# The first of five input pieces projected without its norm, and the norm applied to its 272 columns as products leave PSUM

## What is computed

```python
def rmsnorm(x, g):
    y = x32 * lax.rsqrt(jnp.mean(x32 * x32, axis=-1, keepdims=True) + EPS)
    return (y * g).astype(x.dtype)

def mixer(h, cos, sin, p):          # h = rmsnorm(input, ln_mix_g)
    proj = h @ p['w_in']
    q, k, v, xr, yg = jnp.split(proj, ...)
    q, k = rope(q), rope(k)         # then windowed attention
    xc = centred_depthwise_conv(xr, ...)   # then two gated scans
...
for l in range(DEPTH):
    h = h + mixer(rmsnorm(h, p['ln_mix_g']), cos, sin, p)
    h = h + hier_moe(rmsnorm(h, p['ln_ffn_g']), p)
```

## Time and profile before

| | us |
|---|---|
| median of 3 runs | 1206.02 (1204.71 to 1206.12) |
| the profiled execution | 1203.64 |
| its span, first to last instruction | 1201.9 |
| TensorE busy | 1151.7 (96%) |
| VectorE / ScalarE busy | 925.4 (77%) / 841.1 (70%) |
| mean granted clock of TensorE | 0.985 |

### The profile page before, as it was taken

One profiled execution on the slowest core, in us unless ns is written; L12 is line 12 of the kernel. 1 busy time (PEld: TensorE's weight loads), 2 busy tenths in 40 slices (PEclk: granted clock), 3 DMA queues, 4 the chain that ended last, 5 costly groups with the idle time before them and its releaser, 6 DMA issues.

```text
span 1201.9 us, 21054 instructions
## 1 busy us (share of the span) xinstructions
PE 1151.7 (96%) x5977; PEld 987.8 (82%) x5977; DVE 925.4 (77%) x1254; ACT 841.1 (70%) x1041; POOL 243.5 (20%) x261
## 2 busy tenths in 40 slices
PE   7999999998999999989999999999999999999992
PEld 6999999977888888877788788888888888888881
DVE  6768887476777778679887965566888888888886
ACT  7538888586666666566777855556877777777775
POOL 2130001100111111122232322222322322322320
PEclk8999999999999999999999999999999999999996
DMA  9540111462333322448999787878999999999978
GB/s 350 200 133 18 44 45 34 108 189 78 99 105 93 85 85 85 189 162 332 402 383 375 285 318 255 300 257 292 387 372 378 379 372 363 380 378 366 395 295 326
DMA packets 73271, 291.23 MB, mean 242 GB/s; under 512 B 15051, under 2 KB 30796, under 8 KB 48642
## 3 DMA queue, kind: packets, MB, share of 16 engines
q1 hardware_dynamic: 53826, 257.42, 56.1%
q0 software_dynamic: 19392, 33.16, 10.9%
HBM read 267.75 MB, written 37.62 MB: 254 GB/s over the span
## 4 chain that ended last, share of the span: by engine, by line
PE 80%; DMA 9%; DVE 5%; issue 2%; ACT 2%; SPq 1%; POOL 0%; DVEq 0%; ACTq 0%; POOLq 0%
PE ps L2451 26%; PE ps L800 14%; PE ps L2494 13%; PE ps L1462 9%; DMA raw_w_gate<-in_w_gate 6%; PE ps L1414 3%; PE ps L822 2%; PE ps L1380 2%; PE ps L2438 2%; PE ps L563 2%; PE ps L1391 2%; PE ps L1440 1%; PE ps L2485 1%; DMA raw_w_up<-in_w_up 1%; ACT g_hi L2557 1%
## 5 line engine op out<-in xcount | busy, mean ns | idle before, releaser
L2661 DVE TENSOR_TENSOR d_lo<-raw_w_down,d_hi 128x2048 fp32r<-128x2048 f32 x62 | 139.8, 2289 | 46.9 <-ACT d_hi L2557 46.9
L2661 DVE TENSOR_TENSOR g_lo<-raw_w_gate,g_hi 128x2048 fp32r<-128x2048 f32 x64 | 144.9, 2289 | 35.3 <-ACT g_hi L2557 35.0
L2661 DVE TENSOR_TENSOR u_lo<-raw_w_up,u_hi 128x2048 fp32r<-128x2048 f32 x64 | 143.8, 2288 | 6.5 <-ACT u_hi L2557 6.3
L2557 ACT ACTIVATE g_hi<-raw_w_gate 128x2048 fp32r<-128x2048 f32 x64 | 120.6, 1912 | 25.1 <-DMA raw_w_gate<-in_w_gate 17.9
L2557 ACT ACTIVATE u_hi<-raw_w_up 128x2048 fp32r<-128x2048 f32 x64 | 120.0, 1910 | 10.3 <-DMA raw_w_up<-in_w_up 10.0
L2557 ACT ACTIVATE d_hi<-raw_w_down 128x2048 fp32r<-128x2048 f32 x62 | 115.9, 1910 | 5.8 <-DMA raw_w_down<-in_w_down 5.8
L2494 PE MATMUL ps<-d_hi,hid_hi 128*128 128x512 f32 x272 | 110.7, 407 | 0.4 <-DVE hid_lo L2690 0.4
L2494 PE MATMUL ps<-d_lo,hid_hi 128*128 128x512 f32 x272 | 106.8, 393 | 0.0
L2494 PE MATMUL ps<-d_hi,hid_lo 128*128 128x512 f32 x272 | 106.4, 391 | 0.0
L800 PE MATMUL ps<-h_hi,w_hi 128*128 128x432 f32 (+2 forms) x304 | 104.8, 345 | 0.8 <-DVE h_lo L634 0.8
L800 PE MATMUL ps<-h_lo,w_hi 128*128 128x432 f32 (+2 forms) x304 | 104.3, 343 | 0.0
(11 more groups left out here) (397 smaller groups left out, 2772.2 us busy)
## 6 DMA issues: line engine op xcount, KB each, us to landing
raw_w_gate<-in_w_gate SPq DMA_DIRECT2D x64, 1024.0 KB, 11.5
raw_w_up<-in_w_up SPq DMA_DIRECT2D x64, 1024.0 KB, 11.9
raw_w_down<-in_w_down SPq DMA_DIRECT2D x62, 1024.0 KB, 11.8
w_raw<-in_w_in SPq DMA_DIRECT2D x14, 512.0 KB, 3.6
xh<-in_x SPq DMA_DIRECT2D x10, 512.0 KB, 3.2
h_dram<-xh SPq DMA_DIRECT2D x10, 512.0 KB, 4.2
u_dram<-u SPq DMA_DIRECT2D x10, 512.0 KB, 4.8
k_win<-k_dram POOLq DMA_DIRECT2D x12, 384.0 KB, 5.5
```

The lines of the kernel that those rows point to most:

```text
L2557: act.activation(hi[c][:, :], raw[c][:, :], ACT.Copy).then_inc(hi_done, 1)
L2661: dve.tensor_tensor(lo[c][:, :], raw[c][:, :], hi[c][:, :].bitcast(F32), ALU.subtract).then_inc(lo_done, 1)
```

## The change

Piece 0 is no longer scaled. ScalarE rounds `h_f * g` directly (`first_hi`), VectorE takes the rest (`first_lo`), and TensorE multiplies these. VectorE keeps the row of rstd for the 272 columns in SBUF (`keep_rstd`, in the first columns of `k_pre`; k itself moves to `feat[:, 1, :]`) and multiplies by it wherever a product's first 272 columns leave PSUM: two of `first_scale`, one `scaled_out_of` for each of the tiles 2 to 11, two of `late_scaled` for tiles 12 and 13. ScalarE's copies of those chunks begin at column 272. Chunk 2 of each tile waits for that tile's `scaled_out`, since it writes the same bank, and so do the third and fourth late products.

The loads start with the transposed input of piece 0 and the weights of tile 0; the token rows come in the order t = 3, 4, 0, 1, 2, 5 and so on (`ORDER` = pieces 1, 0, 2, 3, 4). On TensorE the transposes move too. Since `first_rstd` lies in memory that mask buffer 0 takes later, the mask of the first block is loaded later, after the first `swap_q`.

```diff
+    ORDER = (1, 0, *range(2, PIECES))
+    TILE_ORDER = [t for c in ORDER for t in tiles_of(c)]
...
-        load_x(0)
-        load_x(1)
-        load_x(2)
+        sp.dma_start(g_rows[:, :], a["mix_col"]).then_inc(xt_arrived[0], 16)
+        load_xt(0)
+        sp.dma_start(w_raw[0][:, :, :], a["w_in"][0]).then_inc(w_arrived[0], 16)
+        load_x(3)
+        load_x(4)
         sp.dma_start(ident[:, :], a["ident"]).then_inc(consts_in, 16)
-        sp.dma_start(g_rows[:, :], a["mix_col"]).then_inc(consts_in, 16)
-        load_xt(0)
-        for f in range(2):
-            sp.dma_start(w_raw[f][:, :, :], a["w_in"][f]).then_inc(w_arrived[f], 16)
-        for c in range(1, PIECES):
+        sp.dma_start(w_raw[1][:, :, :], a["w_in"][1]).then_inc(w_arrived[1], 16)
+        load_xt(1)
+        for t in tiles_of(0):
+            load_x(t)
+        for c in range(2, PIECES):
             load_x(2 * c + 1)
             load_x(2 * c + 2)
             load_xt(c)
...
+        def first_hi(j):
+            for k in range(HALVES[j].start, HALVES[j].stop):
+                ins = act.activation(h_hi[:, k, piece_cols(0)], h_f[:, k, piece_cols(0)], ACT.Copy, scale=g_rows[:, k:k + 1])
+            ins.then_inc(h_hi_done, 1)
...
-        for t in tiles_of(0):
-            norm(t, t % 2)
-        for j in range(2):
-            split_w(j, j, 0)
-            hi_half(0, j)
+        act.wait_ge(xt_arrived[0], xt_count(0))
+        first_hi(0)
+        split_w(0, 0, 0)
+        first_hi(1)
         for t in tiles_of(1):
-            norm(t, t % 2)
+            norm(t)
+        split_w(1, 1, 0)
         for c in range(1, PIECES):
-            if c >= 2:
+            if c >= 3:
                 first_output(c - 2, 0)
+            if c == 1:
+                norm(0)
+                norm(1)
+                for j in range(2):
+                    hi_half(c, j)
+                norm(2)
...
+    def late_scaled(dve, j):
+        f, bank, _ = late_at(j)
+        dve.wait_ge(proj_out, PUT - len(LATE) + j + 1)
+        dve.tensor_tensor(feat[:, 2 * FT - FTILES + f, META:FIRST_END], bank[:, 0:FIRST_END - META], first_rstd[:, META:FIRST_END],
+                          ALU.mult).then_inc(scaled_out, 1)
...
+        def first_lo(j):
+            dve.wait_ge(h_hi_done, done(j))
+            for k in range(HALVES[j].start, HALVES[j].stop):
+                cols = piece_cols(0)
+                ins = dve.scalar_tensor_tensor(out=h_lo[:, k, cols], in0=h_f[:, k, cols], scalar=g_rows[:, k:k + 1],
+                                               in1=h_hi[:, k, cols].bitcast(F32), op0=ALU.mult, op1=ALU.subtract)
+            ins.then_inc(h_lo_done, 1)
+
+        def keep_rstd():
+            dve.wait_ge(x_turned, done(ORDER.index(0)))
+            dve.tensor_copy(first_rstd, tr[0][:, 0, 0:FIRST_END]).then_inc(first_scaled, 1)
+
+        def first_scale(f):
+            dve.wait_ge(proj_done, f + 3)
+            dve.wait_ge(first_scaled, 1)
+            dve.tensor_tensor((k_own, v_pre)[f][:, 0:FIRST_END], ps[:, FIRST_BANKS[0][f], 0:FIRST_END], first_rstd,
+                              ALU.mult).then_inc(first_scaled, 1)
+
+        def scaled_out_of(f):
+            s = f % 2
+            bank = ps[:, (NCH * s) % 2, :]
+            if f in WITH_META:
+                ft = (f - X0) // 2
+                dve.wait_ge(proj_out, NCH * f + 3)
...
+                dve.tensor_tensor(one(xr, ft, 2 + OFF1, 2 + OFF1 + META), bank[:, 0:META], first_rstd[:, 0:META], ALU.mult)
+                dve.tensor_tensor(one(xr, ft, 2, 2 + FIRST_END), bank[:, 0:FIRST_END], first_rstd, ALU.mult).then_inc(scaled_out, 1)
+            else:
+                scaled_feat(dve, f, bank)
...
         def tile(f, s):
...
                 pe.wait_ge(proj_out, NCH * f + c + 1)
+                if c == 2:
+                    pe.wait_ge(scaled_out, scaled_by(f))
                 third(s, c, (NCH * s + c) % 2, cols=tile_cols(f, c))
...
-        spread(0)
         first_piece(0)
         spread(1)
         first_piece(1)
+        spread(0)
+        piece(0, 1)
         spread(2)
-        for c in range(1, PIECES):
-            for f in range(2):
-                piece(f, c)
-            if c + 2 < PIECES:
-                spread(c + 2)
+        piece(1, 1)
+        for c in range(2, PIECES):
+            piece(0, c)
+            if c + 1 < PIECES:
+                spread(c + 1)
+            piece(1, c)
         tile(X0, 0)
...
         def first_step():
+            projected["late_scaled"](dve, 0)
+            projected["late_scaled"](dve, 1)
             rope_q(0, 0)
```

More of the change, by code:

```diff
@@ L429, in put @@
                 cols = tile_cols(FTILES - 1, c)
-                return act.activation(feat[:, j, cols], bank[:, 0:cols.stop - cols.start], ACT.Copy)
+                lo_ = FIRST_END if c == 0 else cols.start
+                return act.activation(feat[:, j, lo_:cols.stop], bank[:, lo_ - cols.start:cols.stop - cols.start], ACT.Copy)
             return put
@@ L438, in put @@
                 if c == 0:
-                    piece(2 + OFF1, bank, 0, META)
-                    return piece(2, bank, 0, CH)
+                    return piece(2 + FIRST_END, bank, FIRST_END, CH - FIRST_END)
                 if c == 1:
@@ L639, in split_w @@
                               ALU.subtract).then_inc(w_lo_done, 1)
[L641 to L646 removed]
+        dve.wait_ge(xt_arrived[0], xt_count(0))
+        first_lo(0)
         split_w(0, 0)
[L648 removed]
+        first_lo(1)
         for t in tiles_of(1):
             spread_rstd(t)
+        split_w(1, 1)
         for c in range(1, PIECES):
             scale_piece(c)
[L653 to L657 removed]
+            if c == 1:
+                spread_rstd(0)
+                spread_rstd(1)
+                lo_half(c, 0)
+                lo_half(c, 1)
+                spread_rstd(2)
+                keep_rstd()
+                for t in tiles_of(2):
+                    spread_rstd(t)
+                first_scale(0)
+            else:
+                if c < PIECES - 1:
+                    for t in tiles_of(c + 1):
+                        spread_rstd(t)
+                lo_half(c, 0)
+                lo_half(c, 1)
+            if c == 2:
+                first_scale(1)
         step = [0]
@@ L699, in convolve @@
                                          in1=conv, op0=ALU.mult, op1=ALU.add).then_inc(conv_step if j < 3 else conv_done, 1)
+                if j == 2 and f:
+                    scaled_out_of(f)
         def split_xc(ft):
@@ L761, in rec_step @@
             split_w(2 * k + X0 + 3 + d, 1 - d)
-            if d == 1 and not (isinstance(k, int) and k == FT - 1):
-                convolve(k + 1)
+            if d == 1 and k < FT - 1:
+                convolve(k + 1, 2 * k + X0 + 3)
+            elif d == 1:
+                scaled_out_of(2 * k + X0 + 3)
             decayed(k, d)
@@ L1175, in _ @@
         sp.wait_ge(projected["proj_out"], put - late + 2)
+        sp.wait_ge(*projected["scaled_out"])
         swap_q(0)
+        sp.wait_ge(*projected["first_tables"])
+        sp.sem_inc(tables_in[0], 32)
+        sp.dma_start(mask[0][:, :], a["masks"][0]).then_inc(tables_in[0], 16)
         tables(1, 1)
@@ L1746, in rope_q @@
             if isinstance(t, int) and t == 0:
-                dve.wait_ge(projected["proj_out"], put - late + 2)
+                dve.wait_ge(*projected["scaled_out"])
+                dve.wait_ge(*projected["first_tables"])
+            else:
+                dve.wait_ge(tables_in[s], tables_of(t, s))
             if isinstance(t, int) and t == 2:
                 dve.wait_ge(projected["proj_out"], put)
-            dve.wait_ge(tables_in[s], tables_of(t, s))
             dve.wait_ge(q_lo_done, t + 1)
```

130 lines of the change are left out of this document (79 added, 51 removed).

## The result

The changed kernel takes 1215.59 us (median of 4 runs, 1214.92 to 1217.65) against 1206.07 of the kernel before (4 runs): ratio 1.0073, 95% interval 1.0054 to 1.0091, slower by 9.5 us. I had forecast 1211.7, in a range of 1207.0 to 1216.0. The direction and the mechanism are as forecast; the time lies at the upper end of the range, 0.4 us inside it, on the rival that I called "the clock falls every time" (1215.6, chance 0.15).

What follows compares the result with a forecast made beforehand. The prediction took the time at which TensorE reaches tile 2 (50.37), unbroken behind it, to decide; +3.9 for the loop, +1.5 clock, +0.3 late products gave +5.7 on 1206.02, 1211.7 us, range 1207.0 to 1216.0.

Steps and rivals of the forecast that it cites:

- the clock falls every time: Rival: half clock behind each gap before pieces 2 to 4, +9.6 us in all, 1215.6 us; chance 0.15.
- The start: Up to piece 2's scaling (27.6): transposed input lands at 7.0, piece 1's first product at 23.1, 2.5 us earlier.
- The loop: Pieces 2 to 4: scaling, rests, tile 0's products, transposes; 8.25 us a turn against 6.08, tile 2 3.9 us late.
- The clock: TensorE's gaps of 2.25 us before pieces 2, 3 and 4: 0.5 us each, 1.5 in all, ends 0 and 5.1.
- The account of tile 2: First product of tile 2: 54.3 from the loop against 50.37, before 1.5 us for the clock.
- the 53 to 57 that I had named as a sign: Sign in the changed kernel's profile: tile 2 starts from 53 to 57 us.
- The late products: End of the stage: third late product waits for VectorE's added multiplication, 0.3 us on the chain, bounds 0 and 0.6.
- The multiplications between scans: VectorE, one or two instructions of about 0.45 us a tile, covered by its wait for ScalarE: cost nothing.
- The mask's later load: Lands long before the first softmax after 241.56; costed at nothing.
- Faster: Rival: start kept, TensorE's transposes don't hold VectorE up; tile 2 at 46.7, 3.7 us earlier, 1202.6 us; chance 0.10.

Runs made afterwards that it cites:

- the order alone: Kernel before, only the transposes of the next piece's norms moved between tile 0's and tile 1's products of each piece: 1216.22 us, ratio 1.0099.
- the run with filled gaps: Changed kernel with 18 unused products of 256 columns ahead of tile 0's products of pieces 2, 3 and 4: 1210.95 us, ratio 1.0042.
- the half-filled one: Changed kernel with 9 unused products of 256 columns ahead of tile 0's products of pieces 2, 3 and 4: 1208.12 us, one run.
- its early place: Changed kernel with the first mask's load put back ahead of the first cosines: 1214.45 us, ratio 1.0073.
- without the loop: Changed kernel, all transposes ahead of the products of the piece before, first piece's norms last: 1204.11 us; with further edits 1204.53, 1200.59 and 1200.88.
- the unused products: Changed kernel, all transposes ahead, norms in ScalarE's gap, 16 unused products ahead of piece 1: 1200.59 us; with three small loads also moved ahead, 1200.88.
- the first: Changed kernel, all transposes ahead of the products of the piece before, first piece's norms behind the other eight: 1204.11 us, ratio 0.9993.
- the second: Changed kernel, all transposes ahead, first piece's norms in ScalarE's gap ahead of the last piece's rounded copies, no unused products: 1204.53 us, ratio 0.9999.
- the run with the transposes put forward: Changed kernel with the transposes for pieces 3 and 4 ahead of tile 0's products of the piece before: 1208.49 us, ratio 1.0021.
- The run with the late scaling moved: Changed kernel with the first late scaling on VectorE ahead of the recurrence's last two multiplications: 1216.01 us, one run.

## Why the prediction was right, and where it was short

*The start.* Right. The transposed input landed at 7.09 (7.0 forecast), 5.86 us after the load's issue began. The landing is 0.7 us above the bound from the two token loads (6.4) and 1.5 us below the one from the full queue (8.6). Piece 0's first product came at 9.88 (9.6), the scaling of piece 1 at 16.90 (16.1; it waited 0.47 us for transposes behind products at half clock, 0.50 from 14 to 16), piece 1's first product at 23.75 (23.1), tile 0's products there took 4.37 (4.2), and piece 2 was scaled at 28.45 (27.6). So 0.85 us late, inside the ends of 25.6 and 29.6.

*The loop.* Right, and shown: the order alone makes it in the kernel before, and undoing it takes it away. The parts that I added up were 8.25 us with products at full clock; with the clock kept, the run with filled gaps has 8.6 and the half-filled one 8.53. Most of the rest is in the 24 products: I took half of 5.68, 2.84, and they take 3.04 in the half-filled run. The gap ahead of piece 4 I put at 2.25 us like the others; it is 1.78, since VectorE has no norms of a later piece to do there.

*The clock.* This is the term that was mis-sized. I took 0.5 us for each gap, inside ends of 0 and 1.7, from the half-clock stretch that two short gaps had brought before. The changed kernel paid 1.56 and 1.58 (4.60 and 4.62 against 3.04) behind the two gaps of 2.44 us and nothing behind the third, of 1.78 (clock 1.00 from 54 to 60). In no run did the 24 products behind such a gap take between 3.1 and 4.2 us. A mean was the wrong form: the price is nothing or most of a half-clock stretch, and behind gaps of this length the stretch came in 15 of 18 cases (last section). The account of tile 2: forecast 54.3 + 1.5 = 55.8, measured 58.96, outside the 53 to 57 that I had named as a sign. The start is 0.85 of the difference, the clock 3.14 − 1.5 = 1.64, the products at full clock 0.4, and the rest, 0.3, is spread over signals.

*The late products.* Right: 0.32 us at the third late product (0.3 forecast), of which the timeline shows 0.17 as idle, and 0.44 at the first scores, between the bounds. That moving the scaling forward gives nothing by itself I had half said: the queries are delayed beside it.

*Rest.* The multiplications between scans cost nothing, as forecast: from tile 2 to the first late product (220.61 and 229.19) it is 170.2 us in both kernels. The mask's later load I costed at nothing, and its early place gave nothing that the time shows.

*The rivals.* "The clock falls every time" had the right time, 1215.6, by nearly the right account (two of three gaps, and a later start), so that its hitting the time is in part luck. "Faster" needed the loop not to be there, and I priced it at 1202.6: without the loop, the kernels take 1204.1 and 1204.5, which their intervals don't tell from the kernel before, and 1200.6 to 1200.9 only with the unused products. In the first, tile 2 waits for work on ScalarE; in the second, half clock at piece 1 takes a part of the early start back.

## What to carry to other kernels

In a pipeline over pieces, look in the engine's own order for the step that releases the next piece: put behind work that itself waits for this piece, it closes a loop, and each turn can cost more than the start gave (here 4 us a turn against a lead of 1.8 at the first product of piece 1). Where TensorE then stands in short gaps, cost the half clock behind a gap as nothing or as a whole stretch (here nothing or 1.3 to 2.1 us on 24 products, behind gaps of 2.3 to 2.5 us), and look whether the products that it slows are in the loop. When such a gap can't be closed, products that nobody uses may be worth their place (here 1210.95 us with them and 1215.59 without).

## What the runs showed of the hardware

A gap of some 2 us on TensorE was mostly followed by half clock here, but not each time. Over the changed kernel, the order alone, and the edits that keep the loop or the wait ahead of piece 1, there are 18 gaps of 2.19 to 2.48 us on TensorE between 20 and 55 us; behind 15 of them products ran at half clock for a while (the lowest granted clock of a 2 us stretch is 0.50 to 0.55), behind 3 they did not (1.00). Of five gaps of 1.77 to 1.80 us two were followed by it (0.50), three were not (1.00). The two of 1.36 and 1.40 in the half-filled run were not (1.00), but two of 0.97 and 0.90 close together were (the run with the transposes put forward, 30.89 and 32.36, clock 0.50 from 34 to 36). So the length of a gap alone does not decide it. The run with the late scaling moved has the changed kernel's order in this stage, and its three pieces show three prices, in its chain of waits:

```profile
23.59 5.12 PE ps L904 x24
...
34.41 4.34 PE ps L904 x24
...
44.46 3.04 PE ps L904 x24
```

5.12 us is the whole of the 24 products at half clock (0.50 in every 1 us stretch from 23 to 29), 4.34 most of them (0.93 from 35 to 36, then 0.50 to 39), 3.04 full clock (1.00 from 44 to 48), behind gaps of 2.28, 2.46 and 2.35 us.
